# Expert stage of a transformer kernel: a first unit of one head, six row buffers free from the start, query projections interleaved with the weighted sums

## What is computed

```python
def one_chunk(xc):                                  # 128 tokens
    q = (xc @ peer_wq).reshape(128, 8, 2, 128)      # 8 heads, 2 halves
    s = jnp.einsum('chpd,hpkd->chpk', q, peer_keys)
    sv, si = lax.top_k(s, 16)
    cand = (sv[..., 0, :, None] + sv[..., 1, None, :]).reshape(128, 8, 256)
    cidx = (si[..., 0, :, None] * 128 + si[..., 1, None, :]).reshape(128, 8, 256)
    top_s, pos = lax.top_k(cand, 16)
    eidx = jnp.take_along_axis(cidx, pos, axis=-1)
    gate = jax.nn.softmax(top_s, axis=-1)
    act = jax.nn.gelu(jnp.einsum('chkd,cd->chk', peer_u[eidx], xc))
    return jnp.einsum('chk,chkd->cd', gate * act, peer_v[eidx])
```

## Time and profile before

| | before |
|---|---|
| median of 3 runs (lowest, highest) | 2882.38 us (2881.6, 2889.46) |
| profiled execution, its own time | 2877.54 us |
| profiled execution, its span | 2875.7 us |
| PE busy / DVE busy / ACT busy / POOL busy | 92% / 46% / 21% / 17% |
| DMA queue of the gathers: share of 16 engines over the span | 22.6%, 269.12 MB |
| gathers (L2942) | 256 |

### The profile page before, as it was taken

How to read it: one execution, slowest core, us unless ns; L and a number is a source line. 1 busy time by engine, 2 the same in 40 slices (tenths; PEclk the granted TensorE clock), 3 DMA queues, 4 the chain that set the end, 5 groups by cost and what they waited for, 6 DMA issues and landing times.

```text
span 2875.7 us, 54491 instructions
## 1 busy us (share of the span) xinstructions
PE 2635.5 (92%) x23492; PEld 1812.0 (63%) x23492; DVE 1317.5 (46%) x2879; ACT 613.5 (21%) x1341; POOL 497.2 (17%) x397
## 2 busy tenths in 40 slices
PE   8999999999999999999999888888999787787877
PEld 6688685568878743444888887888878333333333
DVE  2873210157531002075374445443414877777655
ACT  1243000014310001023223443333001211111111
POOL 0000000000000000000004344331001554545552
PEclk9999999999999999999999999999999899888899
DMA  5323334343234345213310000000335999999997
GB/s 195 149 89 121 143 149 159 147 162 118 88 121 172 146 169 222 92 74 146 132 59 1 2 3 2 2 2 32 154 146 220 373 421 421 421 421 421 422 421 315
DMA packets 55633, 507.01 MB, mean 176 GB/s; under 512 B 6176, under 2 KB 6176, under 8 KB 7840
## 3 DMA queue, kind: packets, MB, share of 16 engines
q0 software_dynamic: 37056, 269.12, 22.6%
q1 hardware_dynamic: 18400, 235.41, 21.4%
HBM read 503.46 MB, written 1.05 MB: 175 GB/s over the span
## 4 chain that ended last, share of the span: by engine, by line
PE 54%; issue 21%; DMA 11%; DVE 9%; ACT 2%; PEld 2%; DVEq 1%; ACTq 0%; POOL 0%; PEldq 0%; POOLq 0%
PE psum L1524 31%; PE psum L517 17%; DMA mem<-weights,mem 11%; DVE mem L2798 3%; PE psum L1991 3%; DVE mem L2299 2%; PEld psum L1524 2%; PE psum L744 1%; PE psum L1934 1%; PE psum L533 1%; DVE mem L2472 0%; DMA mem<-vectors 0%; PE psum L1534 0%; ACT mem L2141 0%; DVEq L2586 0%
## 5 line engine op out<-in xcount | busy, mean ns | idle before, releaser
L1524 PE MATMUL psum<-mem 64*64 64x64 f32 (+6 forms) x17432 | 1011.2, 258 | 77.9 <-DVEq L2586 19.4
L1524 PEld LDWEIGHTS psum<-mem 64*64 64x64 f32 (+3 forms) x17432 | 790.5, 148 | 294.9 <-issue 199.0
L517 PE MATMUL psum<-mem 128*128 128x256 f32 (+9 forms) x4228 | 968.1, 399 | 4.2 <-ACTq L801 2.1
L517 PEld LDWEIGHTS psum<-mem 128*128 128x128 f32 (+4 forms) x4228 | 708.5, 183 | 256.2 <-issue 168.3
L1991 PE MATMUL psum<-mem 128*128 128x512 f32 x1024 | 504.8, 653 | 131.2 <-ACT mem L2282 131.2
L1991 PEld LDWEIGHTS psum<-mem 128*128 128x128 f32 x1024 | 209.8, 210 | 425.6 <-issue 248.2
L2942 POOL DMA_INDIRECT mem<-weights,mem x256 | 314.7, 1229 | 560.7 <-PE psum L1991 283.5
L2798 DVE CUSTOM_DVE_ANT_0 mem<-mem 128x1024 f32<-128x1024 f32 x256 | 307.9, 1224 | 138.7 <-DMA mem<-weights,mem 132.8
L2850 POOL TENSOR_TENSOR mem<-mem 128x512 f32<-128x512 f32 (+2 forms) x116 | 162.6, 1419 | 683.2 <-PE psum L1524 511.4
L2299 DVE TENSOR_TENSOR mem<-psum,mem 128x512 f32<-128x512 f32 (+1 forms) x224 | 151.1, 685 | 277.9 <-PE psum L1524 244.6
L2299 DVE TENSOR_TENSOR mem<-mem 128x512 f32<-128x512 f32 (+6 forms) x213 | 146.1, 694 | 105.0 <-ACTq L2049 82.7
(11 more groups left out here) (240 smaller groups left out, 1355.8 us busy)
## 6 DMA issues: line engine op xcount, KB each, us to landing
mem<-weights SPq DMA_DIRECT2D x100, 2048.0 KB, 7.3
mem<-weights SPq DMA_DIRECT2D x7, 1024.0 KB, 4.8
mem<-weights SPq DMA_DIRECT2D x2, 2176.0 KB, 8.2
mem<-weights,mem POOLq DMA_INDIRECT x256, 22.2
mem<-weights SPq DMA_DIRECT2D x2, 1536.0 KB, 7.9
mem<-weights SPq DMA_DIRECT2D x2, 1152.0 KB, 8.5
mem<-weights SPq DMA_DIRECT2D x2, 1120.0 KB, 4.9
mem<-x SPq DMA_DIRECT2D x1, 1024.0 KB, 6.1
```

Of the source, the lines that this page charges most:

```text
L517: ins = pe.matmul(out, lhsT, rhs, start=start, stop=stop, skip_group_check=skip)
L1524: ins = pe.matmul(out, lhsT, rhs, start=start, stop=stop, skip_group_check=skip)
```

## The change

- **Units.** The unit of heads 0 and 1 of tile 0 is cut in two units of one head, so there are nine (`UNITS`): slots 0 to 15, 16 to 31, and then 32 each. `rank`, `pair_up`, `rank_pairs`, `look_up`, `choose` and `expert_gates` take a unit's number and work on one head or two.
- **Buffers.** Some small tensors move to other places (`sv` and `peer_out` to the unused ends of the three weight slots, `cand` and `eqb` to constants that are no longer used, `siu` next to the first buffer). That makes room for six buffers that are free at once in place of four, 16 in all. A table `buf_of` gives the buffer of each slot: slots 0 to 23 take buffers 0 to 7 three times (six free at once and two behind group 1), slots 24 to 43 take 8, 9 and 0 to 7 twice, and from slot 44 all 16 go round.
- **TensorE.** After `queries(1)` comes `key_scores(1)` at once. The projections of groups 2 and 3 are cut into chunks (`query_chunk`, a quarter each), one after each group of four sums: sums of group 0, chunk, sums of group 1, chunk, and so on; scores of group 2 after the sums of group 4, scores of group 3 after those of group 9.
- **ScalarE.** Its evacuations follow the same order between the diagonals (`slot_weights`). The first exponential moves in between the two evacuations of group 1.
- **VectorE.** `expert_gates(1)` comes before the first `weigh_slots`; the later units are chosen after groups with `b % 8` of 0, 1, 2 and 4.
- Two semaphores are merged into others (`rows_landed` into `x_landed`, `keys_landed` into `lora_landed`).

The diff, cut to its core:

```diff
-    free_at_once = [base + 2560] + [ptop[0] + 2 * D * i for i in range(3)]
+    free_at_once = [base, base + 2560] + [ptop[0] + 2 * D * i for i in range(4)]
...
+    first_bufs = [*range(8)] * 3 + [8, 9, *range(8)] * 2
+    cycle = [*range(8, 16), *range(8)]
+    buf_of = (first_bufs + cycle * (TT * P // NBUF))[:TT * P]
...
-    UNIT = 32
+    UNITS = [(0, 0, 1), (0, 1, 1)] + [(t, h, 2) for t in range(TT) for h in range(0, 8, 2) if (t, h) != (0, 0)]
+    UNIT_AT = {P * t + 16 * h: u for u, (t, h, n) in enumerate(UNITS)}
...
         queries(1)
-        queries(2)
         key_scores(1)
-        queries(3)
+        for c in range(4):
+            sums([c])
+            query_chunk(2, c)
+        sums([4])
         key_scores(2)
+        for c in range(4):
+            sums([5 + c])
+            query_chunk(3, c)
+        sums([9])
         key_scores(3)
-        for n in range(TT * P):
...
+        sums(range(10, len(SLOT_GROUPS)))
...
-        queries(1)
-        queries(2)
-        key_scores(1)
-        queries(3)
-        key_scores(2)
-        key_scores(3)
...
-        expert_gates(0)
-        expert_gates(1)
-        for b, (first, end) in enumerate(SLOT_GROUPS):
...
+        query_pair(1, 0)
+        expert_gates(0)
+        query_pair(1, 1)
+        expert_gates(1)
+        key_scores(1)
+        slot_weights([0, 1, 2])
+        query_pair(2, 0)
+        slot_weights([3, 4])
+        query_pair(2, 1)
+        slot_weights([5])
+        key_scores(2)
+        slot_weights([6, 7])
+        query_pair(3, 0)
+        slot_weights([8, 9])
+        query_pair(3, 1)
+        slot_weights([10])
+        key_scores(3)
+        slot_weights(range(11, len(SLOT_GROUPS)))
...
         for u in range(2):
-            rank(0, u)
-            pair_up(0, u)
-            rank_pairs(0, u)
-            choose(0, u)
+            rank(u)
+            pair_up(u)
+            rank_pairs(u)
+            choose(u)
         expert_gates(0)
+        expert_gates(1)
         v.wait_ge(*h2_ready.at(0, 1))
         for b in range(len(SLOT_GROUPS)):
             weigh_slots(b)
-            step, ahead = b % 8, b // 8 + 2
...
-            if b == 0:
-                expert_gates(1)
-            if ahead < 8:
-                if step == 1:
...
-                elif step == 3:
...
-                elif step == 5:
...
-                elif step == 7:
...
+            ahead = b // 8 + 2
+            if ahead < len(UNITS):
+                if b % 8 == 0:
+                    rank(ahead)
+                elif b % 8 == 1:
+                    pair_up(ahead)
+                    rank_pairs(ahead)
+                elif b % 8 == 2:
+                    choose(ahead)
+                elif b % 8 == 4:
                     expert_gates(ahead)
...
         for n in range(TT * P):
-            if n % UNIT == 0:
-                pool.wait_ge(*experts_ready.at(0, n // UNIT))
+            if n in UNIT_AT:
+                pool.wait_ge(*experts_ready.at(0, UNIT_AT[n]))
+            m, at = user_before[n], row_at[buf_of[n]]
             for g in (1, 2, 3):
-                if n < NBUF and row_at[n] == behind_query[g][0]:
+                if m is None and at == behind_query[g][0]:
                     pool.wait_ge(*qTp_ready.at(0, g + 1))
-            if n < NBUF and row_at[n] == behind_scores[0]:
+            if m is None and at == behind_scores[0]:
                 pool.wait_ge(*scores_ready.at(0, 2 * 4 - 1))
-            if n >= NBUF:
-                pool.wait_ge(*rows_summed.at(0, n - NBUF))
+            if m is not None:
+                pool.wait_ge(*rows_summed.at(0, m))
```

More of the change, by code:

```diff
@@ L1941, in queries, with query_chunk, sums @@
             channel_major(act_ring, "qp", hT, km_view(item(f"wq{g}"), 512), 8, 4)
+        def query_chunk(g, c):
+            if c == 0:
+                query_weights[g] = km_view(item(f"wq{g}"), 512)
+            if c % 2 == 0:
+                query_bank[0] = act_ring.open(pe, "qp")
+            for k in range(8):
+                last = mm(query_bank[0][:, (c % 2) * T:(c % 2 + 1) * T], query_weights[g][:, k, c * P:(c + 1) * P], hT[:, k, :], k == 0, k == 7)
+            if c % 2 == 1:
+                last.then_inc(act_ring.full, 1)
+        query_bank = [None]
+        query_weights = {}
+        def sums(groups):
+            for b in groups:
+                for n in range(*SLOT_GROUPS[b]):
+                    t, k = divmod(n, P)
+                    pe.wait_ge(*diag_ready.at(0, n))
+                    for half in range(2):
+                        last = pe.matmul(psum[:, 4 + 2 * t + half, :], diag[:, n % DIAGS, :],
+                                         rows_uv[buf_of[n]][:, D + half * 512:D + (half + 1) * 512], start=k == 0, stop=k == P - 1)
+                        if half == 1 or n == TT * P - 1:
+                            last.then_inc(rows_summed.sem, 1)
         def score_products(b, g, t):
@@ L2236, in first_queries, with query_pair @@
             act.drain().then_inc(qTp_ready.sem, 1)
[L2238 to L2241, removed]
+        def query_pair(g, pair):
+            c = 4 * g + 2 * pair
+            done(A(qTp[:, c:c + 2, :], take("qp").rearrange("p (c t) -> p c t", c=2), ACT.Copy))
+            if pair:
+                act.drain().then_inc(qTp_ready.sem, 1)
         def key_scores(g, tiles=range(TT)):
@@ L2258, in _, with slot_weights @@
         h2_copies(1)
-        queries(1)
-        queries(2)
-        key_scores(1)
-        queries(3)
-        key_scores(2)
-        key_scores(3)
         def expert_gates(u):
-            t, g = divmod(u, 4)
-            y = gatep[:, t, 2 * g:2 * g + 2, :]
+            t, h, n = UNITS[u]
+            y = gatep[:, t, h:h + n, :]
             act.wait_ge(*gate_shift_ready.at(0, u))
             A(y, y, ACT.Exp).then_inc(gate_exp_ready.sem, 1)
+        def slot_weights(groups):
+            for b in groups:
+                first, end = SLOT_GROUPS[b]
+                s = slice(first, end)
+                act.wait_ge(*gelu_in_ready.at(0, b))
+                A(g1[:, s], g1[:, s], ACT.Tanh, scale=float(np.sqrt(2.0 / np.pi))).then_inc(gelu_tanh_ready.sem, 1)
+                act.wait_ge(*slot_weights_ready.at(0, b))
+                for n in range(first, end):
+                    if n >= DIAGS:
+                        act.wait_ge(*rows_summed.at(0, n - DIAGS))
+                    A(diag[:, n % DIAGS, :], ident, ACT.Copy, scale=g1[:, n:n + 1]).then_inc(diag_ready.sem, 1)
+                if b % 8 == 3 and b // 8 + 2 < len(UNITS):
+                    expert_gates(b // 8 + 2)
+        query_pair(1, 0)
         expert_gates(0)
+        query_pair(1, 1)
         expert_gates(1)
-        for b, (first, end) in enumerate(SLOT_GROUPS):
[L2275 to L2284, removed]
+        key_scores(1)
[12 more added lines that the diff above has]
+        slot_weights(range(11, len(SLOT_GROUPS)))
         act_ring.check("post")
```

138 lines of the change are left out of this document (69 added, 69 removed).

## The result

| | before | changed |
|---|---|---|
| median (lowest, highest), 5 runs each | 2882.38 us (2878.18, 2889.46) | 2862.92 us (2861.04, 2871.79) |
| ratio, 95% interval | | 0.9932 (0.9908 to 0.9955) |
| span of the profiled execution | 2875.7 us | 2861.1 us |
| first instruction of `rank`, unit 0 | 2182.82 | 2184.68 |
| from there to the end of the span | **692.9** | **676.4** |

The change is faster by 0.7%. The last row is the cleaner measure. What lies ahead of `rank` is the same work in both (only semaphores and the places of small tensors differ), yet it took between 2182.2 and 2198.3 us in the twelve executions profiled for this study. So I count the stage from the first instruction of `rank` on, written **+t** from here. The stage became 16.5 us shorter; a second profile of the changed kernel gave 676.3.

The account below looks back on a forecast made before the run. Gathers on the DMA engines bound the expert stage at 2.533 us a slot. (7 x 2.533) - 0.4 = 17.3 us; 2877.54 - 17.3 = 2860.2, with 4.8 for the median 2865.1 us; range 2858 to 2876.

Parts of the forecast that it names:

- The bound: Expert stage: gathers set it, with the DMA engines busy all the time at 421 GB/s, 2.533 us a slot.
- The start: Unit 0 with one head: first gather at about 2193.2, 6.2 us earlier; sharing with the last weight item taken as nothing.
- The ring of eight: Groups 0 to 3: slot n + 8 goes out when slot n is summed; slot 23 lands at about 2261.5.
- in time: Ring of eight: a burst of four is late only if issued more than 11.0 us after the one before.
- the last burst: Group 3, gather 20: lands 2253.0 where 2251.9 was due, 1.1 late; with the wait at its head slot 23 at 2261.5.
- One every 1.75 us: From gather 8, after the first sum: gathers go out one every 1.75 us, to 2220.4.
- dry bursts: Rival, ring of eight: late bursts from slow issues and one fall of PE's clock; gain 10.2 us, 2872.2; chance 0.20.
- From slot 24 on: Slots 24 to 49: no lull but thin cover; PE 69.9 against DMA 70.9 us over slots 16 to 43.
- the slower rival: PE's clock falls in the mixed stretch, slots 0 to 43: 13 us slower, 2895; chance 0.08.
- The sum: Whole kernel: slot 23 at 2261.5 against slot 16 at 2261.1 before, (7 x 2.533) - 0.4 = 17.3 us gained.

Follow-up runs that it names:

- ring of six: Changed kernel with a ring of six in place of eight buffers for slots 0 to 23; median 2891.2 us, ratio 1.0024 to the kernel before.
- one chunk ahead: Changed kernel with each query chunk of group 2 ahead of a group of sums: ratio 0.9935; in a second kernel also later units' choice spread: 0.9939.
- projections first: Changed kernel with all projections and scores of groups 2 and 3 ahead of the first sum; median 2895.4 us, ratio 1.0038.
- two chunks ahead and the first choice spread: Changed kernel with two query chunks of group 2 ahead of the first sums, unit 2 chosen behind groups 1, 3, 5 and 6; 2867.8 us, ratio 0.9939.

## Why the prediction was right

**The bound** held: 421 GB/s and share 1.01 from 2258 on; from slot 49 to 255 it is 521.5 us for 206 slots, 2.532 a slot against the 2.533 of the prediction; and two buffers fewer change nothing.

**The start.** 10.1 us from `rank` to the expert numbers was predicted; gather 0 came at +10.5 where +10.4 stood. Slot 0 landed after 6.6 us, not 5.7: 0.9 of the 0 to 2 us left open for sharing with the last weight item, taken as nothing. Little of it lasted: slot 3 landed at +24.8 where +24.6 was predicted, slot 7 at +34.7 as predicted.

**The ring of eight.** On the prediction's clock, less 2182.82:

| | predicted | measured |
|---|---|---|
| gather 8 | +32.3 | +32.9 |
| gather 12 | +42.8 | +43.3 |
| gather 16 | +53.1 | +54.1 |
| gather 20 | +64.5 | +65.5 |
| gather 24 | +74.2 | +74.8 |
| slot 11 landed | +46.5 | +47.7 |
| slot 15 landed | +56.6 | +59.0 |
| slot 19 landed | +66.6 | +69.3 |
| slot 23 landed | +78.7 | +80.5 |

The times at which gathers 8 to 24 went out were right to 1.0 us. The step that was a little off is what follows from them, "in time": bursts 12 and 16 were taken to land at the steady pace, since each went out less than 11.0 us after the one before. They did go out in time by that rule, and still slots 15 and 19 landed 2.4 and 2.7 us late. At slot 23 only 1.8 us of this are left, because the prediction had charged some 2 us of its own to the last burst. Issue to landing of slots 15, 19 and 20:

```profile
DMA to landing us min/median/max: 9.5/9.5/9.5
...
DMA to landing us min/median/max: 10.0/10.0/10.0
...
DMA to landing us min/median/max: 7.1/7.1/7.1
```

Gather 20 is the clearest case: it went out 6.3 us before it was due (slot 19 at +69.3, plus 2.5), more than the 5.7 us of a gather at an idle queue, and landed 7.1 us after its issue, 0.8 late. So 5.7 us of lead does not keep the queue full; this fits the 378 GB/s of the ring of eight at share 0.99. Why so few gathers in flight move less, no run here shows.

One part of it may be slow issues. "One every 1.75 us" took the gathers to be issued at the pace of the sums; in the changed kernel gathers 13 and 14 took 1.96 and 1.98 us each to issue, so that 15 went out 6.3 us after 12 where 5.25 was counted, and slot 15 landed 3.3 us behind slot 14 in place of 2.5:

```profile
2229.65 1.96 POOL L2992 DMA_INDIRECT mem<-weights,mem  x1 [0.77 <-PE psum L1970]
2231.91 1.98 POOL L2992 DMA_INDIRECT mem<-weights,mem  x1 [0.30 <-issue]
2234.20 0.95 POOL L2992 DMA_INDIRECT mem<-weights,mem  x1 [0.30 <-issue]
```

But gathers 18 and 19 were as slow (1.97 and 1.99 us) and their slots landed at the steady pace. The mechanism of the rival "dry bursts" is so borne out in part, and its price was a quarter of what it charged: 1.8 us at slot 23 in place of 7.1. No run held the issues quick to see what is left.

**From slot 24 on** the cover was as thin as written. Slot 49 landed 7.7 us after its issue, 2.5 behind slot 48; against the 5.7 us of an idle queue that is 2.0 us of slack, where about 3 had been counted. TensorE's waits were 1.34 us at most from its first sum to 2318, where one of 2.07 began, and the clock stayed at 1.00 from 2217 to 2296, so the slower rival did not come. The ring of six shows that its mechanism is real: there the estimate that left it out was 15 us too low.

**The sum.** 17.3 us predicted, 16.5 measured in the stage; the medians moved by 19.5, more than the stage, within the scatter of what lies ahead of it. 2865.1 was predicted, 2862.9 measured. The last 1.2 us between slot 49 (15.3) and the end (16.5) have no step of the prediction. That stretch took 531.9 us in the profiled execution of the kernel before and 530.7 in that of the changed one, both inside the 530.1 to 532.0 of all ten: what brings 15.3 close to the 17.3 is luck in these 1.2 us. The steps of the prediction themselves were 2.0 us too good.

## What to carry to other kernels

Where a stage is bound by transfers, count in units of the transfer: which one has landed at a given time, before and after, times the steady pace. An early start and the buffers behind it are worth something only together: the small unit was worth 0 us alone and about 5 with the ring, the ring without the interleaving made the kernel slower. A ring that is only just long enough by the sum of its times loses a little all the same: leave more lead than a transfer at an idle queue takes. Work that has to be done anyway on TensorE is best put one piece into each gap, not all into the first one: it hides there and keeps the clock up: two of four pieces put ahead of the first gap left a later gap of 4.9 us open, and the stage became 2.4 us longer.

## What the runs showed of the hardware

- **GpSimd takes nearly twice as long to issue a gather while VectorE multiplies.** I compared each of the 256 issues of the changed kernel with the multiplications of 1024 columns (L2849) in the trace. Of 45 issues that met none in their first 0.94 us, the mean duration was 0.95 us and the longest 1.11; of 68 whose first 0.94 us were covered by them throughout, the mean was 1.72 and the longest 1.99. In the kernel before it was 0.98 (67 issues, the longest 1.37) and 1.67 (62). VectorE's other work does not do this: 31 of the 45 issues had it beside them for over 80% of that time, and their mean was 0.95 too. These rows of VectorE lie over the two slow issues shown above:

```profile
2229.56 1.23 DVE L2849 CUSTOM_DVE_ANT_0 mem<-mem 128x1024 f32<-128x1024 f32 x1
...
2230.72 1.22 DVE L2849 CUSTOM_DVE_ANT_0 mem<-mem 128x1024 f32<-128x1024 f32 x1
...
2231.86 1.22 DVE L2849 CUSTOM_DVE_ANT_0 mem<-mem 128x1024 f32<-128x1024 f32 x1
```

  It is a correlation over the trace, and not every covered issue is slow (the shortest took 0.94 us); no run took the multiplication away. The Trainium skill (SBUF — State Buffer, "SBUF: two separate sides") names two-port modes of VectorE as what starves a GpSimd DMA of descriptors; whether this multiplication runs in one, no run here shows.
- **Waits of 2.6 to 3.4 us on TensorE sometimes cost its clock and sometimes not.** With one chunk ahead TensorE waited 3.38 us before the first sum in two kernels; in one, 16 instructions took 7.13 us with the granted clock at 1.00 (2221.7 to 2228.7), in the other 8.81 with the clock at 0.57 in the first 4 us (2212 to 2216). After 2.63 us they took 10.21 in the ring of six (above), after 2.77 us 7.13 with two chunks ahead and the first choice spread:

```profile
2254.38 7.13 PE L1970 MATMUL psum<-mem 128*128 128x512 f32 x16 [2.77 <-ACT mem L2309]
```

  After waits of 1.50 us (the same kernel), 1.87 (projections first) and 2.18 (the kernel before) they ran at full clock.
- **At the end the DMA engines are nearly idle for about nine microseconds while the last slots land.** In the changed kernel the share is 0.09 in the first window below and 0.06 in the second, and slot 255 lands at 2851.9. In the kernel before the share is 0.06 too from 2859 to 2865, and slot 255 lands at 2866.5. One sixteenth is 0.06, so it looks as if one of the 16 engines were late and worked alone; this was not tried.

```profile
2843.00:2850.00 7.00, 5.74 (x14) 2.39 (x13) 5.23 (x19) 2.11 (x7) 0.00 (x0) 1.00 0.09 36
...
2845.00:2851.00 6.00, 6.00 (x15) 2.65 (x16) 4.67 (x16) 1.31 (x5) 0.00 (x0) 1.00 0.06 26
```
